# Moving an expert's down-projection weights from SyncE's DMA queue to ScalarE's, in a mixture-of-experts layer

## What is computed

```python
def moe_ffn(h, w_router, b_router, w_gu, b_gu, w_down, b_down):
    logits = h @ w_router + b_router
    top_val, top_idx = lax.top_k(logits, TOP_K)          # 4 of 32
    gates = softmax(top_val)
    ...                                                  # rows sorted by expert
    def step(acc, blk):
        tok, gate, e = blk
        xb = h[tok]
        gu = xb @ w_gu[e] + b_gu[e]                      # 1024 -> 2048
        x_glu, x_lin = split(gu, 2)
        ...                                              # clamps
        act = x_glu * sigmoid(1.702 * x_glu) * (x_lin + 1.0)
        out = (act @ w_down[e] + b_down[e]) * gate       # 1024 -> 1024
        return acc.at[tok].add(out), None
```

## Time and profile before

| | |
|---|---|
| three runs, median (lowest to highest) | 1291.8 us (1289.81 to 1294.97) |
| the profiled execution's own time | 1288.81 us |
| its span, first to last instruction | 1286.9 us |
| mean granted TensorE clock | 0.948 |
| TensorE matmul busy | 1128.0 us (88%) |
| VectorE, ScalarE busy | 378.3 us (29%), 200.6 us (16%) |
| bytes moved, mean rate | 454.87 MB, 353 GB/s |
| chain that ended last | PE 73%, DMA 14%, DVE 5% of the span |

### The profile page before, as it was taken

One profiled execution on the slowest core, in us unless ns is written; L12 is line 12 of the kernel. 1 busy time (PEld: TensorE's weight loads), 2 busy tenths in 40 slices (PEclk: granted clock), 3 DMA queues, 4 the chain that ended last, 5 costly groups with the idle time before them and its releaser, 6 DMA issues.

```text
span 1286.9 us, 20473 instructions
## 1 busy us (share of the span) xinstructions
PE 1128.0 (88%) x6676; PEld 508.5 (40%) x6677; DVE 378.3 (29%) x1044; ACT 200.6 (16%) x419; POOL 46.2 (4%) x28
## 2 busy tenths in 40 slices
PE   4999998967887888799999988989999999879894
PEld 0666564643232232244333444444333333224441
DVE  2133735342332222212422123123222233221233
ACT  2323242141110101101111011011111111100100
POOL 0141101020000000000000000000000000000000
PEclk9999999986998999898999999999999999989997
DMA  9963229623999999999999999989999999999991
GB/s 380 346 233 135 67 91 373 258 79 115 420 421 422 422 422 422 422 422 397 413 421 422 422 354 424 422 345 424 422 421 422 422 422 421 423 422 422 407 396 45
DMA packets 76913, 454.87 MB, mean 353 GB/s; under 512 B 9900, under 2 KB 14764, under 8 KB 24556
## 3 DMA queue, kind: packets, MB, share of 16 engines
q1 hardware_dynamic: 70336, 449.76, 85.6%
q10 hardware_dynamic: 6540, 4.60, 1.3%
HBM read 451.17 MB, written 3.17 MB: 353 GB/s over the span
## 4 chain that ended last, share of the span: by engine, by line
PE 73%; DMA 14%; DVE 5%; issue 4%; ACT 2%; SPq 1%; DVEq 0%; POOL 0%; ACTq 0%
PE psum L863 28%; PE psum L891 15%; DMA ring<-w_gu 10%; PE psum L563 6%; PE psum L910 5%; PE psum L772 3%; PE psum L832 2%; PE psum L572 2%; DMA ring<-w_down 2%; DMA ring<-w_ada 2%; PE psum L840 1%; PE psum L527 1%; PE psum L856 1%; DVE work L1589 1%; DVE work L1593 1%
## 5 line engine op out<-in xcount | busy, mean ns | idle before, releaser
L863 PE MATMUL psum<-ring,work 128*32 128x512 f32 (+2 forms) x2048 | 427.4, 616 | 28.7 <-DMA ring<-w_gu 27.9
L863 PEld LDWEIGHTS psum<-ring,work 128*32 128x32 f32 (+2 forms) x2048 | 131.5, 133 | 275.9 <-issue 202.3
L891 PE MATMUL psum<-ring,work 128*32 128x256 f32 (+2 forms) x1504 | 218.5, 478 | 9.7 <-DMA ring<-w_down 6.9
L1604 DVE TENSOR_TENSOR work<-psum,work 128x320 f32<-128x320 f32 x256 | 110.0, 485 | 228.5 <-PE psum L910 227.5
L967 ACT ACTIVATE work<-psum 128x256 f32<-128x256 f32 (+6 forms) x207 | 88.6, 445 | 356.2 <-PE psum L891 220.6
L891 PEld LDWEIGHTS psum<-ring,work 128*32 128x32 f32 (+2 forms) x1504 | 98.0, 129 | 114.9 <-issue 95.0
L1574 DVE TENSOR_SCALAR work<-csb 96x128 bf16<-96x128 f32 x64 | 15.4, 280 | 407.8 <-PE psum L863 406.9
L1223 ACT ACTIVATE work<-work 128x128 f32<-128x128 f32 (+2 forms) x64 | 25.2, 393 | 562.2 <-DVE work L1588 560.9
L563 PE MATMUL psum<-h,ring 128*128 128x320 f32 x320 | 91.3, 443 | 1.2 <-ACT h L1002 1.2
L910 PE MATMUL psum<-work 32*128 32x320 f32 (+2 forms) x512 | 82.1, 481 | 1.1 <-ACT work L967 1.0
L832 PE MATMUL psum<-work 128*32 128x256 bf16 (+4 forms) x846 | 67.2, 318 | 6.7 <-DVE work L1562 3.6
(11 more groups left out here) (212 smaller groups left out, 640.3 us busy)
## 6 DMA issues: line engine op xcount, KB each, us to landing
ring<-w_gu SPq DMA_DIRECT2D x256, 1024.0 KB, 18.9
ring<-w_down SPq DMA_DIRECT2D x128, 1024.0 KB, 17.8
ring<-w_ada SPq DMA_DIRECT2D x12, 2048.0 KB, 9.3
ring<-w_in SPq DMA_DIRECT2D x7, 2048.0 KB, 29.9
ring<-w_out SPq DMA_DIRECT2D x2, 2048.0 KB, 12.0
x<-xT SPq DMA_DIRECT2D x1, 1280.0 KB, 6.0
yT<-h SPq DMA_DIRECT2D x4, 320.0 KB, 2.2
work<-b_exp ACTq DMA_DIRECT2D x3, 384.0 KB, 16.4
```

The source lines that it names most:

```text
L863: last = mm(o, xg[:, kk, 0:m], cols(ring[:, kk, :]), start=False, stop=kk == KD - 1)
L891: last = mm(o, actT[:, kk, 0:m], ring[:, GU_UNITS + kk // 2, c1_:c1_ + n], start=False, stop=kk == 7)
L1604: tt_(t_, bank[SPREAD_BANKS[u]][:, 0:T], t_, ALU.add).then_inc(acc_ready, 1)
```

## The change

SyncE keeps the eight gate and up loads of every expert but the first. The four down loads of expert e+1 are issued by ScalarE on ScalarE's own queue, all four in a row, behind the instruction that copies expert e's output, and before ScalarE's wait for the scatter weights. They have no wait of their own: the copy's wait for the fourth `dn_used` of expert e stands ahead of them. Expert 0's loads stay as they were, and the last expert issues none. The loads of a second pass are changed in the same way.

```diff
-            def load_expert(e, turn):
-                for j, (dst, src) in enumerate(expert_units(e)):
+            def load_gate_up(e, turn):
+                for j, (dst, src) in enumerate(expert_units(e)[0:GU_UNITS]):
                     sp.wait_ge(*used_unit(j, turn - 1))
                     sp.dma_start(dst, src).then_inc(unit_full[j], 16)
 
             with sp.Fori(1, NE) as e:
-                load_expert(e, e)
+                load_gate_up(e, e)
...
+            def load_down(e):
+
+                for j in range(GU_UNITS, UNITS):
+                    dst, src = expert_units(e)[j]
+                    act_.dma_start(dst, src).then_inc(unit_full[j], 16)
+
             def start(turn, e, b):
+                if not isinstance(b, int):
+                    load_down(e)
                 by_size(act_, count(act_, e), b, lambda groups: (gathered(turn, groups), turned(turn, groups)))
...
                 by_size(act_, n, b, lambda groups: outputs(turn, groups))
+                if not ends:
+                    load_down(e + 1)
                 act_.wait_ge(str_ps, turn + 1)
                 copy(spread, bank[1][:, 0:T]).then_inc(spread_ready, 1)
```

More of the change, by code:

```diff
@@ L492, in _ @@
                     with sp.Fori(0, NE) as e:
-                        load_expert(e, b * NE + e)
+                        load_gate_up(e, b * NE + e)
             yv = yT.rearrange("(k p) t -> p k t", p=P)
```

## The result

The changed kernel takes 1357.42 us (median of 4 runs, 1350.26 to 1359.3), the kernel before in the same comparison 1292.01 us: 1.0498 times as long, 95% interval 1.0459 to 1.0538. The forecast was 1353 us, its range 1307 to 1368. The profiled execution of the changed kernel takes 1356.08 us with a span of 1354.2 us.

What follows compares the result with a forecast made beforehand. DMA engines bound the kernel, losing time while the ring is full. Last load: 313.0 + 925.2 + 4.2 + 72.9 = 1315.3 us; 33.1 more gives span 1348.4, 61.5 more than before; median 1353 us, range 1307 to 1368.

Steps and rivals of the forecast that it cites:

- The account in DMA time: Whole kernel: 372 units at 2.487 us plus 15.6 us wasted while the ring is full put the last load at 1253.8.
- the four dips: Ends of the four big experts: DMA engines idle 72.9 us (67.9 to 77.8), replacing 15.6 us before.
- the gap at the beginning: Expert 1's gate-up units are through at 332.9 us, down loads begin at 337.1: 4.2 us idle.
- nothing changes: Rival: same bytes, and the late start of down loads hides in the remaining queue; 1292 us, chance 0.04.
- Between these places I count no idle time: Small and medium experts leave the DMA engines behind as before, so no idle time is added there.
- the units: Work left for DMA at each big expert: 20.5 units, ends 20 and 21, where one queue had 24.
- the clock: TensorE slower behind runs of waits: nothing to 2.5 us at each big expert, up to 10, only in the range.
- Halves of the rate: Where both queues hold work, engines take packets by turns, so each queue gets half the rate.
- one line after all: Rival: engines serve loads in issue order across queues, only the late start counts; 1309 us, chance 0.11.
- ScalarE's issues: Four loads at 0.42 us each, hidden, cost 0; rival: 3.08 us each delays `spread`, 1391 us, chance 0.04.
- down weights land earlier than they are needed: With two queues, down weights land early and gate-up weights of the same expert later, by itself wasting no DMA time.
- faster: Rival: TensorE's 6.9 us of waits for down weights end; 1285 us, chance 0.03.

Runs made afterwards that it cites:

- half-row run: Changed kernel with each down unit brought by two loads of 4 KB rows instead of one of 8 KB rows: 1410.38 us, ratio 1.0929.
- the late start alone: Kernel before, SyncE issuing all loads on one queue, but each down load waits for the expert's last down unit: 1312.94 us, ratio 1.0145.
- the second queue alone: Changed kernel, but ScalarE waits for each down buffer and issues its load at once, ahead of the output copy: 1328.13 us, ratio 1.0256.
- mending those four: Changed kernel, but behind big experts only ScalarE issues each down load as its buffer comes free: 1326.56 us, ratio 1.024.
- mending all 31: Changed kernel, but at every expert ScalarE issues each down load as its buffer comes free: 1328.13 us, ratio 1.0256.
- the two runs that mix them: Changed kernel with down units as two 4 KB-row loads: 1410.38 us; the same with the issues behind the copy to `spread`: 1417.22 us, ratio 1.0977.

## Why the prediction was right

**What sets the time.** The account in DMA time held, and by place: the four dips and the gap at the beginning take 74.7 + 4.8 us of DMA time, 64.2 more than the four dips took before, where the sum had 61.5. The copies and SyncE's queue do not enter. The rival "nothing changes" falls with the ratio of 1.0498.

**The idle stretches.** Predicted 72.9 us at four places, 67.9 and 77.8 as ends; measured 74.7 with the edges, 68.6 of them without any traffic. At the beginning 4.2 were predicted and 4.8 lost. "Between these places I count no idle time" held: 422 GB/s there. By place the forecast was worse than in sum: its own terms give 17.7, 21.0, 17.1 and 17.0 us, measured are 21.6, 19.2, 19.4 and 14.6, and the fourth stretch without traffic, 13.3 us, is shorter than the 16 to 20 named as a sign. That the sum came so near is in part luck, for errors of either sign met in it. One is the units: 20.6 and 20.5 at the first and the third place, as counted, but 21.8 at the fourth, where a down unit of the expert before was still under way (TensorE waited for it until 1222.08 us). The other is the clock, which the sum left out and the range allowed up to 2.5 us in each stretch. From the last awaited unit to the end of the big expert's down matmuls the first place took 69.3 us (66.1 predicted), the third 67.8 (65.5), the fourth 66.4 (65.4). At the first, the start is the row at 559.35 us above, behind a wait of 3.89 us; the clock that followed, and the end:

```profile
555.00:565.00 10.00, 5.78 (x22) 1.54 (x18) 1.86 (x8) 0.62 (x2) 0.00 (x0) 0.51 1.01 419
...
612.88 15.80 PE L891 MATMUL psum<-ring,work 128*128 128x512 f32 x32
```

The granted clock was 0.51 there, the lower of the two levels (1.2 GHz), where the kernel before had 1.00 in the same place of its order (545 to 555 us). The third place had 0.50 from 835 to 840 us; the fourth had 1.00, so its 1.0 us has another cause. At the second place the last awaited unit came one expert earlier, at 697.65 us, so that its length cannot be compared. At the third, the prediction's start "having waited for it" had no row: the kernel before shows no wait of TensorE for weights between 696 and 1030 us.

**Halves of the rate.** Shown by 222 and 230 packets, by the 4.97 us a unit, and by the half-row run, in which the shares followed the rows' length. The rival "one line after all" falls; its price of 1309 us was nearly that of the run which has one line and the late start (1312.94).

**Late start and second queue together.** The prediction gave one sum for both. The runs split it: the late start alone costs 1.45%, the second queue alone 2.56%, both 4.98%, a little more than the sum of the two; why more was not looked for. The late start counts behind the four big experts, as its term said: mending those four was worth as much, within the noise, as mending all 31.

**ScalarE's issues.** Predicted 0.42 us each and hidden; they took 0.34 us each (median), the four 2.05 us with what lies between them, and no wait of TensorE for the copies was added. Moving the loads behind the copy to `spread` gained nothing. The rival falls.

**Waits for the weights.** The signs named ahead were more waits at L863 and hardly any at L891. The first came (52.2 us, 27.9 before); the second did not: 27.0 us at L891, 6.9 before. The sentence "down weights land earlier than they are needed" is the step that failed, in small experts. In one of them ScalarE issues the four loads from 366.14 us on, and TensorE reaches the down units 14.2 us later, at 380.31; but four units at half the rate take 4 x 4.97 = 19.9 us. The last two come late, 4.97 us apart:

```profile
385.10 1.94 PE L891 MATMUL psum<-ring,work 128*32 128x256 f32 x16 [2.86 <-DMA ring<-w_down]
390.07 1.93 PE L891 MATMUL psum<-ring,work 128*32 128x256 f32 x16 [3.04 <-DMA ring<-w_down]
```

It does not change the sum, since the DMA engines run at their full rate meanwhile (422 GB/s from 345 to 600 us). The rival "faster" rested on those waits going away.

**The end.** TensorE begins the last gate-up unit when it lands, at 1319.86 us (predicted 1315.3), and 34.3 us follow (predicted 33.1):

```profile
1319.86 3.61 PE L863 MATMUL psum<-ring,work 128*64 128x512 f32 x8 [3.05 <-DMA ring<-w_gu]
```

The unit took 3.61 us where the one ahead of it, behind a wait of 2.28 us, took 1.94. The granted clock was 0.52 from 1320.0 to 1323.4 us, the lower level (1.2 GHz), behind the wait of 3.05 us: the cost of waits that the prediction named but had no row to price.

## What to carry to other kernels

Where the DMA engines are the limit, count a change in DMA time that is wasted: find the stretches in which a ring of buffers is full, and ask how many units of work are queued when one begins and when the next load can be issued. One queue in the order of need was worth something in itself here (2.56%), since a second queue takes its turns whether its data is needed next or not, and what it brings early is missing when the engines would otherwise have run ahead. Loads issued as a batch behind the last use of their buffers cost nothing measurable where other loads were queued; where none were, at four places, they cost some 30 us with two queues and 19 with one.

## What was not expected of the hardware

Rows of 4 KB instead of 8 KB cost 1% of the rate on one queue (418 and 422 GB/s in the same window), and with 8 KB rows in the other queue more in places: 409 and 388 GB/s from 400 to 580 us in the two runs that mix them, 415 from 940 to 1110 us in the first of these. The cause was not looked for.
